# Fifteen of the sixteen up-product groups of the first MLP with channels on partitions, and the norm's root applied once, squared, at the residual

## The reference, cut to what matters

```
h = rms_norm(x, norm_mlp)                       # x: 256 x 2048; h = (x * gain) * rstd per token
x = x + square(relu(h @ w_up)) @ w_down         # w_up 2048 x 8192, w_down 8192 x 2048
```

## Time and profile before

| what | us |
|---|---|
| median of 3 runs | 2589.48 (2587.59 to 2591.14) |
| profiled execution, its own time | 2588.87 |
| its span | 2587.1 |
| PE busy | 2568.3 (99%) |
| PEld busy | 2140.5 (83%) |
| DVE busy | 1847.9 (71%) |
| ACT busy | 1371.9 (53%) |

### The profile page before, as it was taken

How to read it: one execution, slowest core, us unless ns; L and a number is a source line. 1 busy time by engine, 2 the same in 40 slices (tenths; PEclk the granted TensorE clock), 3 DMA queues, 4 the chain that set the end, 5 groups by cost and what they waited for, 6 DMA issues and landing times.

```text
span 2587.1 us, 34184 instructions
## 1 busy us (share of the span) xinstructions
PE 2568.3 (99%) x12494; PEld 2140.5 (83%) x12494; DVE 1847.9 (71%) x3348; ACT 1371.9 (53%) x2637; POOL 277.8 (11%) x353
## 2 busy tenths in 40 slices
PE   9999999999999999999999999999999999999999
PEld 7988888888888888888888888888788888888887
DVE  6678666777899999676867875677866665555555
ACT  7355575655545445465766565564544444444443
POOL 1011100012122232300011110000001111000000
PEclk9999999999999999999999999999999999999999
DMA  8796665688899998977777755444577777666665
GB/s 297 239 303 188 208 201 171 196 283 279 292 296 291 297 303 286 280 227 226 233 235 235 247 166 165 143 142 149 163 232 258 258 256 221 183 195 191 188 191 160
DMA packets 187064, 587.10 MB, mean 227 GB/s; under 512 B 40688, under 2 KB 40720, under 8 KB 186768
## 3 DMA queue, kind: packets, MB, share of 16 engines
q1 hardware_dynamic: 156608, 559.94, 66.3%
q0 software_dynamic: 30000, 24.66, 5.2%
q10 hardware_dynamic: 288, 0.31, 0.0%
HBM read 574.33 MB, written 2.10 MB: 223 GB/s over the span
## 4 chain that ended last, share of the span: by engine, by line
PE 95%; ACT 2%; DVE 1%; DMA 1%; issue 1%; SPq 0%; ACTq 0%; DVEq 0%
PE ps L1885 26%; PE ps L1887 26%; PE ps L1886 26%; PE ps L1863 5%; PE ps L1864 2%; PE ps L1806 2%; PE ps L1955 1%; PE ps L1925 1%; PE ps L1944 1%; DVE wlo L2547 0%; DMA x<-in_x 0%; ACT whi L2194 0%; DMA raw<-in_w_in_h 0%; PE ps L2070 0%; DMA raw<-in_w_in 0%
## 5 line engine op out<-in xcount | busy, mean ns | idle before, releaser
L2547 DVE TENSOR_TENSOR wlo<-raw,whi 128x512 fp32r<-128x512 f32 x1712 | 1097.3, 686 | 520.0 <-ACT whi L2194 518.2
L2194 ACT ACTIVATE whi<-raw 128x512 fp32r<-128x512 f32 x1712 | 981.5, 624 | 800.5 <-PE ps L1887 534.8
L1885 PE MATMUL ps<-whi,thl 128*128 128x512 f32 (+1 forms) x3122 | 1228.2, 393 | 3.2 <-ACT hA L2385 1.0
L1887 PE MATMUL ps<-whi,thl 128*128 128x512 f32 (+1 forms) x3122 | 1210.4, 388 | 0.0
L1886 PE MATMUL ps<-wlo,thl 128*128 128x512 f32 (+1 forms) x3122 | 1209.1, 387 | 0.0
L1885 PEld LDWEIGHTS ps<-whi,thl 128*128 128x128 f32 x3122 | 586.6, 188 | 122.5 <-issue 4.1
L1887 PEld LDWEIGHTS ps<-whi,thl 128*128 128x128 f32 x3122 | 586.2, 188 | 121.4
L1886 PEld LDWEIGHTS ps<-wlo,thl 128*128 128x128 f32 x3122 | 586.9, 188 | 116.1 <-issue 1.0
L2565 DVE SCALAR_TENSOR_TENSOR acc<-raw,silc,acc 128x512 f32<-128x512 f32 x480 | 343.9, 746 | 8.1 <-DMA raw<-in_w_mod 3.6
L1783 POOL DMA_DIRECT2D acc<-acc x168 | 133.8, 796 | 1343.2 <-DVE acc L2565 784.1
L1863 PE MATMUL ps<-thl,whi 128*128 128x512 f32 x576 | 207.4, 403 | 5.6 <-DVE wlo L2547 3.8
(11 more groups left out here) (342 smaller groups left out, 1401.7 us busy)
## 6 DMA issues: line engine op xcount, KB each, us to landing
raw<-in_w_down SPq DMA_DIRECT2D x216, 512.0 KB, 3.8
raw<-in_w_mod SPq DMA_DIRECT2D x192, 512.0 KB, 4.3
raw<-in_w_gate_up SPq DMA_DIRECT2D x176, 512.0 KB, 3.6
raw<-in_w_in SPq DMA_DIRECT2D x175, 512.0 KB, 3.6
raw<-in_w_up SPq DMA_DIRECT2D x128, 512.0 KB, 4.5
raw<-in_w_out SPq DMA_DIRECT2D x64, 512.0 KB, 3.6
raw<-in_w_in_h SPq DMA_DIRECT2D x56, 512.0 KB, 5.1
raw<-in_w_in_tail SPq DMA_DIRECT2D x16, 268.0 KB, 4.4
```

The costliest lines, as they stand in the source:

```text
L1885: pe.matmul(p, xh, wh[:, c, c0:n], start=a and (form != "both" or tb == 0), stop=False, skip_group_check=True)
L1887: ins = pe.matmul(p, xl, wh[:, c, c0:n], start=False, stop=z, skip_group_check=True)
L2194: self.e.activation(t.his[g % NHI][:, at], t.raws[j % NRAW][:, at], ACT.Copy).then_inc(*s.hi.up((g, c // u)))
L2547: self.e.tensor_tensor(t.los[j % NRAW][:, at], t.raws[j % NRAW][:, at], t.his[g % NHI][:, at].bitcast(F), ALU.subtract).then_inc(*s.lo.up( ...
```

## The change

The weights `w_up` are laid out in two arrays: the first 512 columns as before, the other 7680 in blocks of 256 columns (`w_up_h`), as the form "heads" wants them. Group 0 of up(0) stays in form "rows" with its transposes; the other 15 groups become two blocks of 256 channels each in form "heads", with a new epilogue in which no transpose stands. rstd is no longer applied at Relu; a new small VectorE instruction squares it once, and the down residual multiplies by it.

```
+    def hidden_heads(self, name, op, kt):
+        s = self.s
+
+        def epi(b, pair, end):
+            def run():
+                while not self.stgs.ready():
+                    yield
+                key, slot = (name, b), self.stgs.take()
+                u = slot.tile[:, 0, :].rearrange("p (h s) -> p h s", h=2)
+                self.heads_joined(name, b, pair, end, u, slot.after)
+                pair.give((s.hj, key))
+                yield
+                self.hidden_square(key, u, op, kt + 2 * b)
+                yield
+                self.hidden_low(key, u, op, kt + 2 * b)
+                for z in range(2):
+                    op.ready[kt + 2 * b + z] = [(s.ul, key)]
+                slot.give((s.ul, key))
+            self.spawn("small", run())
+        return epi
...
         opm.rs = self.sums("mlp", 12)
-        self.opm = opm
+        self.norm_squared(opm)
...
             for i in range(4):
-                self.gemm(opm, w_up, 0, 2048 * b + 512 * i, 512, range(16), self.hidden(("up", b, i), op, 4 * i, None))
+                if b or i:
+                    self.gemm(opm, a["w_up_h"], 0, 2048 * b + 512 * i - 512, 512, range(16), self.hidden_heads(("up", b, i), op, 4 * i), "heads")
+                else:
+                    self.gemm(opm, w_up, 0, 0, 512, range(16), self.hidden(("up", b, i), op, 4 * i, None))
...
-                self.gemm(op, w_down, 2048 * b, 512 * n, 512, range(16), self.residual(f"dn{b}", n, last=b == 3))
+                self.gemm(op, w_down, 2048 * b, 512 * n, 512, range(16), self.residual(f"dn{b}", n, last=b == 3, scaled=True))
...
-            self.e.activation(slot.tile[:, tb, :], pair.tile[tb][:, :], ACT.Relu, **self.scaled(self.opm, tb)).then_inc(*self.s.u0.up((key, tb)))
+            self.e.activation(slot.tile[:, tb, :], pair.tile[tb][:, :], ACT.Relu).then_inc(*self.s.u0.up((key, tb)))
...
+    def hidden_square(self, key, u, op, kt):
+        s, ac = self.s, self.e
+        self.wait_ge(*s.hj.at(key))
+        ac.activation(u, u, ACT.Relu).then_inc(*s.u0.up(key))
+        self.wait_ge(*s.u0.at(key))
+        ac.activation(u, u, ACT.Square).then_inc(*s.u1.up(key))
+        self.wait_ge(*s.u1.at(key))
+        self.wait_all(op.used)
+        ac.activation(op.h[:, kt:kt + 2, :], u, ACT.Copy).then_inc(*s.uh.up(key))
...
+        if scaled:
+            self.wait_ge(*s.rs2.at(0))
+            self.wait_all(self.xb[2 * n + tb])
+            dv.scalar_tensor_tensor(out=x, in0=pair.tile[tb][:, :], scalar=t.rs2[:, tb:tb + 1], in1=x, op0=ALU.mult,
+                                    op1=ALU.add).then_inc(*s.res.up(key))
+            return
...
+    def norm_squared(self, op):
+        t, s = self.t, self.s
+        self.wait_ge(*s.rs.at("mlp"))
+        rs = t.st[:, 12:14]
+        self.e.tensor_tensor(t.rs2[:, :], rs, rs, ALU.mult).then_inc(*s.rs2.up(0))
+
+    def hidden_low(self, key, u, op, kt):
+        s = self.s
+        self.wait_ge(*s.uh.at(key))
+        self.e.tensor_tensor(op.l[:, kt:kt + 2, :], u, op.h[:, kt:kt + 2, :].bitcast(F), ALU.subtract).then_inc(*s.ul.up(key))
...
+    laid["w_up"], laid["w_up_h"] = packed(inputs["w_up"][0][:, 0:512]), packed(inputs["w_up"][0][:, 512:], 256)
```

More of the change, by code:

```diff
@@ L131, in __init__ @@
         self.gx, self.gs = new("mod_gain_1"), new("mod_gain")
+        self.rs2 = new("mlp_rstd_squared")
         self.fn, self.gr, self.gcp = new("final_scaled"), new("gate_spread"), new("gate_copied")
@@ L315, in __init__ @@
         self.ps = [nc.alloc_psum_tensor(f"ps{i}", [128, 512], F) for i in range(8)]
-        self.ssm, self.rn = small("ssm", [2, 4]), small("rn", [2, 8])
+        self.ssm, self.rn, self.rs2 = small("ssm", [2, 4]), small("rn", [2, 8]), small("rs2", [2])
         self.gain = {n: self.cols[:, 16 * i:16 * i + 16] for i, n in enumerate(("mix", "xa", "mem", "mlp", "mix2", "ffn2"))}
@@ L362 @@
     cmp_blocks = cmp_hidden = cmp_parts = cmp_fold = cmp_gelu = cmp_second = cmp_probs = skip
-    hidden_out = hidden_turn = silu_out = prod_out = mod_gain = final_scale = final_square = gate_row = skip
+    norm_squared = hidden_square = hidden_low = hidden_out = hidden_turn = silu_out = prod_out = mod_gain = final_scale = final_square = gate_row = skip
     bound_diff = gate_sigmoids = gate_scale = gate_keys = gate_logs = forget_b = forget_c = ctx_state = scan_ones = head_turned = head_states = head_outputs = skip
@@ L827, in spread, with residual @@
         self.spawn("small", run())
-    def residual(self, st, n, last=False, gate=False, out=False, halves=False):
+    def residual(self, st, n, last=False, gate=False, out=False, halves=False, scaled=False):
         def epi(pair, end):
@@ L837, in epi @@
                     slot = self.stgs.take()
-                self.residual_add(key, pair, (s.mh, end[1]) if halves and tb == 0 else end, slot, last, out)
+                self.residual_add(key, pair, (s.mh, end[1]) if halves and tb == 0 else end, slot, last, out, scaled)
                 if gate:
@@ L1693, in issue, with residual_add @@
         sp.dma_start(view(t.raws[j % NRAW], shape), src).then_inc(*s.raw[j % NRAW].up(j, 16))
-    def residual_add(self, key, pair, end, slot, last, out):
+    def residual_add(self, key, pair, end, slot, last, out, scaled):
         if out:
@@ L3018 @@
         'k_norm_g_2', 'attn_sink_2']
-_WEIGHTS = ['w_out', 'xattn_wkv', 'xattn_wo', 'w_up', 'w_down', 'w_mod_2', 'w_in_2', 'w_out_2', 'w_gate_up_2',
+_WEIGHTS = ['w_out', 'xattn_wkv', 'xattn_wo', 'w_down', 'w_mod_2', 'w_in_2', 'w_out_2', 'w_gate_up_2',
             'w_down_2']
```

## The result

| | us, median | ratio to before, with its 95% interval |
|---|---|---|
| before | 2588.53 (2586.75 to 2591.14) | |
| the change | 2602.91 (2602.61 to 2603.43) | 1.0057 (1.0045 to 1.0068) |

The change makes the kernel 14.4 us slower; 2587.6 us was forecast, with a range up to 2593.5. The profiled execution took 2602.73 us, its span 2600.9.

A forecast was written before the change was run, and what follows sets the result against it. TensorE was taken as the bound, with VectorE 3 to 5 us per part behind. From 2588.87 us, -14.4 (transposes) + 12.8 (dearer chunks) + 0.3 (stalls) = -1.3 gave 2587.6 us; range 2580.5 to 2593.5.

The forecast's parts named there:

- Transposes gone: TensorE, MLP up parts: 15 groups lose their transposes at 0.96 us each, 14.4 us gained, all on the path.
- The dearer chunk: TensorE, up parts: 120 chunks in form "heads" at 2.827 us instead of 2.720, 12.8 us lost; 6.4 at the fast pace.
- The residual: VectorE, down parts: scaled residual 0.5 us dearer per part, 1.0 in the loaded ones; squaring the root taken as 0.
- loads: Weight loads of the new up array: same 512 KB per chunk, landing in 3.6 us against 4.5; 0 either way.
- pairs: A block's two banks, returned after the join, are wanted by PE only four chunks (11 us) later; 0.
- The epilogue: ScalarE, up parts: four more copies, 1.5 us per group; no added wait, splits needed 8.5 us later; nothing on the path.
- The VectorE step: VectorE, loaded parts: joins and residual give 5.3 us of arrears, mostly covered by the splits' lead; 0.3 us of PE stalls.
- Rival D: up(2) and up(3): VectorE becomes the bound once arrears exceed the lead; costs 5.3 to 13.4 us, 2596.3 us; chance 0.12.

The follow-up runs named there:

- e1: The changed kernel with Relu, Square and rounding (and VectorE's low part) one chunk later; 2586.35 us, ratio 0.9995.
- e7: e1 with two fp32 transposes of the identity on TensorE ahead of each up part's first block in form "heads"; 2583.63 us, ratio 0.9982.
- e4: Only the change's scaled residual (Relu unscaled, squared root at the down residual), all 16 groups in form "rows" with transposes; 2587.65 us, ratio 1.0000.
- e9: e1 with each "heads" chunk in two passes, first the 8 matmuls of 512 columns, then the 8 of 256; 2579.89 us, ratio 0.9970.
- e3: The changed kernel with the modulation's rate 0.46 instead of 0.5, its work spread over more chunks; 2609.73 us, ratio 1.0085.
- e6: The changed kernel with Relu, Square and rounding one chunk earlier, directly behind VectorE's join; 2624.44 us, ratio 1.0140.
- e10: e9 with group 0 of up(0) in form "heads" too, so all sixteen groups have it; 2591.41 us, ratio 1.0012.

## Why the prediction was wrong

Point by point. **Transposes gone**, -14.4 us: right; where nothing else happens a group takes 22.6 us in place of 22.7 with them. **The dearer chunk**, +12.8 us at the slow pace: right, 0.3534 us per pair against 0.3533 forecast; the sum of the two, -1.6 us, is what e1 shows within the MLP (-1.8 us by the ends of the chunks). That part of the change has next to no gain to give, and TensorE's side of it was forecast to 0.2 us. That all four parts took the slow pace was in part luck: e7 gives two of them the fast one with one small edit. **The residual**, `norm_squared`: right (e4); loads, pairs: right (no wait of PE in the loaded parts of e1).

**The epilogue** is the step that failed, in one clause: "`heads_joined` ... adds no wait of its own. ... Nothing on the path." It looked at ScalarE's copies, which indeed wait for nothing new, and at the length of the burst of three passes, and did not ask what Relu waits for. Before, ScalarE waited for TensorE in this epilogue (line 2366), and VectorE for ScalarE, never ScalarE for VectorE. The change adds that third edge, with the splits of the next chunks queued behind it. Any lag of VectorE behind ScalarE then turns into a wait of ScalarE, and this into a new wait of VectorE: 1.35 us per block, blocks of 12.82 us in place of 11.31, and 15.6 us lost in up(2) and up(3) with the chunks behind them, where the sum had 0.3.

The VectorE step, 5.3 us of arrears over 270, was a little high as load: it reckoned 13.4 us more work, while VectorE's busy time in the three windows rose from 257.9 to 266.3 us in e1, and PE lost none of it. Rival D named the right place and parts and the right point of decision, and had 13.4 us as its upper end, near the 15.6 that were lost and still under them. But the waits for ScalarE that it counted as time that VectorE "could not use" were those there already, not the ring, so the nearness of its number is luck; and it got 0.12, on the argument that PE had no wait there before. That only said that the lead had covered all so far, when the change was about to spend it. With the third edge seen, the 1.35 and 2.5 us per block were there to be reckoned beforehand: the prediction's burst of 1.9 us and one split on ScalarE (0.62 us in the trace before) make 2.5, and less one pair of `wlo` (2 x 0.6 us) 1.3.

The version to keep is e1 with e9's two passes: 0.3% under the kernel before. Not tried: the same with the modulation slightly slower and its last scatter in time.

## What to carry to other kernels

When a step moves an operation to another engine, draw for each new instruction whom it waits for and what is queued behind it on its own engine, and look for a ring of engines that run at a lag to each other: where each engine carries out its stream in order, a lag turns into a wait that feeds itself. A late engine that still has free time in the trace (8 of 94 us here) is the sign of one. The ring costs something only where the late engine has no room (e3), and here the remedy cost nothing: the waiting instruction written one chunk later, behind the work that the other engine needs (e1).

## What the runs showed of the hardware that I had not expected

- The same matmuls cost differently by their order. Long and short ones alternating (512, 256 columns) run at 0.3533 or 0.3466 us per pair, each pace stable for some 250 pairs (up(2) of e1, up(3) of e7); 512, 512, 256, 256 runs at 0.3483 us (2.787 us per chunk) everywhere; 8 and 8 at 0.349. I have no cause for it, and what puts a stretch into one pace or the other stays open: two transposes ahead (e7) did so in some parts and not in others. The code of the stretch does not decide it: in the product of the earlier trace rows, which e1 leaves as it was, 64 pairs of e1 lie between

```profile
161.31 0.39 PE L1889 MATMUL ps<-thl,whi 128*128 128x512 f32 x1
...
183.49 0.39 PE L1889 MATMUL ps<-thl,whi 128*128 128x512 f32 x1
```

  0.3466 us each, where the kernel before, the changed one and e6 take 0.3534. So some 0.4 us between two of these kernels can be this alone.
- VectorE can be 98 to 100% busy by the windows without TensorE losing anything (e1).
- A stall of PE can cost more than its length: the granted clock went to 0.50 during or right behind PE's waits and the matmuls behind them ran at it (27.3 us at 0.50 in e3, 6.8 in e10; in e6 four times 3.4 us, three of them behind waits of 2.2 to 2.6 us).
